# Both down projections as Strassen products over chunks of tile pairs

## The reference, cut to what matters

```
# first block, D_FF = 2816
x = x + (silu(h @ w_gate) * (h @ w_up)) @ w_down
x = rms_norm(x, final_norm)          # then second block's first rms_norm
# second block, D_FF_2 = 4096
f = square(relu(h @ w_ff1)) @ w_ff2
return x + rms_norm_2(f, g_post_ffn)
```

## Time and profile before

| | |
|---|---|
| median of 3 runs | 2897.8 us (2894.25 to 2903.49) |
| the profiled execution | 2899.71 us, of which the span of instructions is 2897.9 us |
| PE busy | 2785.0 us, 96% of the span, 13622 matmuls |
| DVE busy | 1349.2 us, 47% |
| POOL busy | 995.2 us, 34% |
| ACT busy | 842.6 us, 29% |
| mean granted PE clock | 0.975 |
| chain that ended last | PE 85%, DVE 6%, POOL 3% |

### The profile page before, as it was taken

The page is one execution under the profiler, slowest core; times in us unless marked ns, Lnnn a source line. Parts: engine busy times, 40 slices in busy tenths (PEclk is TensorE's granted clock), DMA queues, the critical chain, the costliest instruction groups (busy, mean ns, idle before and its releaser), DMA issues.

```text
span 2897.9 us, 34574 instructions
## 1 busy us (share of the span) xinstructions
PE 2785.0 (96%) x13622; PEld 2330.2 (80%) x13622; DVE 1349.2 (47%) x2385; ACT 842.6 (29%) x1584; POOL 995.2 (34%) x746
## 2 busy tenths in 40 slices
PE   7999999999999999999999899999996999999998
PEld 6767888777887888888788678989876888878887
DVE  4352111251233644444556621157627666656666
ACT  4352111122222423323121511057624233321121
POOL 2121100243233456555623432235244434322221
PEclk9899999999999999999999999989998999999999
DMA  4101220101341122222522122122023333333223
GB/s 164 49 34 45 90 71 32 62 15 48 107 170 66 67 87 79 81 88 99 214 88 95 67 75 67 40 63 60 19 96 99 99 115 111 134 141 108 96 88 102
DMA packets 104175, 248.28 MB, mean 86 GB/s; under 512 B 17829, under 2 KB 36901, under 8 KB 103845
## 3 DMA queue, kind: packets, MB, share of 16 engines
q1 hardware_dynamic: 104014, 246.07, 25.6%
HBM read 192.18 MB, written 53.59 MB: 85 GB/s over the span
## 4 chain that ended last, share of the span: by engine, by line
PE 85%; DVE 6%; POOL 3%; ACT 2%; issue 2%; DMA 1%; SPq 0%; POOLq 0%; DVEq 0%; ACTq 0%
PE PS L658 8%; PE PS L660 8%; PE PS L661 8%; PE PS L455 7%; PE PS L456 7%; PE PS L457 7%; PE PS L681 6%; PE PS L682 6%; PE PS L683 6%; PE PS L775 3%; PE PS L471 3%; PE PS L473 3%; PE PS L472 3%; PE PS L752 1%; PE PS L540 1%
## 5 line engine op out<-in xcount | busy, mean ns | idle before, releaser
L1781 POOL TENSOR_TENSOR WL<-WRAW,WH 128x1024 fp32r<-128x1024 f32 (+1 forms) x154 | 296.9, 1930 | 1063.2 <-ACT WH L828 1063.1
L828 ACT ACTIVATE WH<-WRAW 128x1024 fp32r<-128x1024 f32 (+1 forms) x262 | 223.6, 865 | 463.5 <-PE PS L683 374.8
L681 PE MATMUL PS<-WH,H1L 128*128 128x512 f32 x800 | 314.0, 393 | 9.9 <-DVE X L1554 9.6
L682 PE MATMUL PS<-WL,H1H 128*128 128x512 f32 x800 | 313.0, 391 | 0.0
L683 PE MATMUL PS<-WH,H1H 128*128 128x512 f32 x800 | 313.0, 391 | 0.0
L1556 DVE TENSOR_TENSOR X<-PS,X 128x512 f32<-128x512 f32 x368 | 242.6, 684 | 144.7 <-PE PS L683 138.4
L455 PE MATMUL PS<-HH,WL 128*128 128x512 f32 x736 | 294.2, 400 | 2.0 <-DVE HL L1268 1.9
L456 PE MATMUL PS<-HL,WH 128*128 128x512 f32 x736 | 291.3, 396 | 0.0
L457 PE MATMUL PS<-HH,WH 128*128 128x512 f32 x736 | 290.5, 395 | 0.0
L658 PE MATMUL PS<-HH,WL 128*128 128x512 f32 (+1 forms) x672 | 251.0, 373 | 8.0 <-DVE HS L1506 4.3
L660 PE MATMUL PS<-HL,WH 128*128 128x512 f32 (+1 forms) x672 | 249.4, 371 | 0.0
(11 more groups left out here) (336 smaller groups left out, 5527.7 us busy)
## 6 DMA issues: line engine op xcount, KB each, us to landing
WRAW<-in_u_f SPq DMA_DIRECT2D x64, 512.0 KB, 3.5
WRAW<-in_u_in SPq DMA_DIRECT2D x50, 512.0 KB, 3.5
HRAW<-scr_h SPq DMA_DIRECT2D x25, 1024.0 KB, 6.0
scr_h<-HS SPq DMA_DIRECT2D x96, 256.0 KB, 2.2
WRAW<-in_u_gu SPq DMA_DIRECT2D x44, 512.0 KB, 3.4
scr_x<-X SPq DMA_DIRECT2D x24, 512.0 KB, 3.0
WRAW<-in_u_dn SPq DMA_DIRECT2D x22, 512.0 KB, 3.5
X<-in_x SPq DMA_DIRECT2D x16, 512.0 KB, 8.4
```

Of the source, the lines that this page charges most:

```text
L681: e.matmul(PS[:, b, :], hl, wh, start=(t == ks[0] and f == 0), stop=False)
L682: e.matmul(PS[:, b, :], hh, wl, start=False, stop=False)
L1781: e.tensor_tensor(lo, raw, hi.bitcast(F32), ALU.subtract).then_inc(*c.inc("w_lo_p", i))
```

## The change

Both down projections become Strassen products. The tile pairs are taken in chunks: 3, 4 and 4 pairs in layer 1, four times 4 in layer 2. The hidden activation of a chunk is a 2x2 matrix of quarters A11 to A22 (rows 0 to 511 and 512 to 1023, first and second tile of each pair), and the weight likewise B11 to B22. For a chunk, SP loads the eight raw quarters straight from memory into `HHF` and `HLF` (the weights of this stage no longer pass through `WRAW`), 128x512 for each pair. POOL makes the eight sums S1 to S4 and T1 to T4 in place, for each pair (only S1 of the first chunk is made by DVE). For each of the seven products P1, P2, P5, P6, P7, P3, P4 and each pair of the chunk, ACT casts A and B (two instructions of 128x512) and DVE subtracts for both (two of 128x512). PE makes 4 groups of 3 matmuls for each pair, accumulated over the chunk in 4 banks. The A slots hold two products, so the split of a product waits until the product two before it is finished. DVE adds the finished banks into `X` or into a helper `DV` (28 additions of 128x512 for a chunk, from PSUM), and POOL adds `DV` into three of the four quarters of `X` and P1 into the fourth (16 instructions of 128x512 for a chunk, 12 in the first chunk of layer 2). In layer 1 the residual is loaded into `X` before. The last two products are made bank by bank, so that row tiles 0 to 3 finish with P3 and 4 to 7 with P4. The norm of layer 1 keeps its multiplication on POOL but has fewer small steps. In layer 2 POOL multiplies the row by the norm's weight (`XG`), and DVE then does scaling and residual in one instruction. The 324 fewer matmuls are 12 for each of 27 pairs.

```diff
+    CHUNKS = {1: [range(0, 3), range(3, 7), range(7, 11)], 2: [range(4 * k, 4 * k + 4) for k in range(4)]}
+    DORDER = ["P1", "P2", "P5", "P6", "P7", "P3", "P4"]
...
+        def ffn_down(lay):                        # PE
+            last = len(STEPS[lay])
+            for n, (k, p) in enumerate(STEPS[lay]):
...
+                    w.wait_ge(*c.at("d_al", (lay, n, i)))
+                    w.wait_ge(*lo_done(op))
...
+                    e.matmul(dst, hl, wh, start=(i == 0), stop=False)
+                    e.matmul(dst, hh, wl, start=False, stop=False)
+                    mm = e.matmul(dst, hh, wh, start=False, stop=(i == g - 1))
...
+                if n < last - 2:
+                    for i in range(g):
+                        for b in range(4):
+                            part(i, b)
+                else:
+                    for b in range(4):
+                        for i in range(g):
+                            part(i, b)
...
+        def d_split(lay, n, items):               # DVE
...
+            for i in items:
+                w.wait_ge(*c.at("d_ah", (lay, n, i)))
+                e.tensor_tensor(d_slot(lay, n, i, 1), d_tile(a_kind, i), d_slot(lay, n, i, 0).bitcast(F32),
+                                ALU.subtract).then_inc(*c.inc("d_al", (lay, n, i)))
+                op = DOP[lay, n, i]
+                w.wait_ge(*c.at("w_hi", op))
+                e.tensor_tensor(half_slot(WL, op), d_tile(b_kind, i), half_slot(WH, op).bitcast(F32),
+                                ALU.subtract).then_inc(*c.inc("w_lo_v", op))
...
+            for n in range(last - 1):
+                g = len(CHUNKS[lay][STEPS[lay][n + 1][0]])
+                for b in range(4):
+                    if n and STEPS[lay][n - 1][1] != "P1":
+                        add(n - 1, b)
+                    d_split(lay, n + 1, range(b, min(b + 1, g)))
...
+                def tile_sum(i, kind, left, right, sign):     # POOL
...
+                    e.tensor_tensor(d_tile(kind, i), d_tile(left, i), d_tile(right, i), sign).then_inc(
+                        *c.inc("d_s", (lay, k, i, kind)))
...
+                        e.tensor_tensor(d_out(q, b), d_out(q, b), DV[:, b, :], ALU.add).then_inc(
+                            *c.inc("d_v", (lay, k, q, b)))
...
+        def fin2(tt):                             # POOL
...
+            e.tensor_tensor(XG[:, tt % 2, :], X[:, tt, :], NG[:, 0, :], ALU.mult).then_inc(*c.inc("n_f", (6, tt)))
             rsqrt(6, tt, VV[1][:, tt:tt + 1], RR[1][:, tt:tt + 1])
...
+        def fin2(s):                              # DVE
+            if 0 <= s - 2 < NT:
+                finish(s - 2)
+            if 0 <= s - 1 < NT:
+                variance(6, s - 1, SS[1], VV[1])
```

More of the change, by code:

```diff
@@ L337, in ready @@
     def ready(i, key):
-        return all(p < NHS or bk.order.get(LAST.get(p - NHS), 1 << 30) <= bk.order[key] for p in places(i))
+        return ops[i][0] != "d" and all(p < NHS or bk.order.get(LAST.get(p - NHS), 1 << 30) <= bk.order[key] for p in places(i))
     def b_tile(kind, n):
@@ L666, in strassen @@
                         turns(k, backs, AFTER_PROD[lay][m][x])
[L668 to L695, removed]
@@ L697, in pe_program @@
         strassen(1, 2, backs)
-        ffn_down(1, FF1, "u_dn")
+        ffn_down(1)
+        for tt in range(4):
+            back(3, tt)
         for half in range(2):
@@ L703, in pe_program @@
                 proj_t(("zu", j, half), U["u_in2", j], half, HH, HL)
-                if half == 0 and j < 3:
-                    back(3, 5 + j)
+            if half == 0:
+                for tt in range(4, NT):
+                    back(3, tt)
         for tt in range(NT):
@@ L1234, in fin2 @@
         def fin2(tt):
-            w.wait_ge(*bk.out(("dl", 2, tt, 0)))
-            w.wait_ge(*bk.out(("dl", 2, tt, 1)))
+            if tt >= NT:
+                return
+            for done in row_done(2, tt):
+                w.wait_ge(*done)
             if tt >= 1:
@@ L2234, in ffn_down @@
             fin(-1)
+            w.wait_ge(*lo_done(DOP[lay, last - 1, len(CHUNKS[lay][-1]) - 1]))
+            feed(d_key(lay, last - 3, 3))
+            feed(d_key(lay, last - 2, 3))
             for tt in range(NT):
[L2236 to L2237 removed]
                 fin(tt)
+            feed(d_key(lay, last - 1, 3))
         def store_x2(tt):
```

580 lines of the change are left out of this document (351 added, 229 removed).

## The result

The changed kernel takes 2956.4 us (median; 2947.6 to 2957.1), the kernel before, in the same session, 2900.6 us: ratio 1.0188, 95% interval 1.0161 to 1.0216. The forecast was 2927 us (slower, 0.72). The direction and the mechanism were right, and the time lies in the range, but the cost was about twice what I forecast: 55.8 us instead of 29.2 (2927 against the 2897.8 us known then).

A forecast was written before the change was run, and what follows sets the result against it. PE alone bound the down stages before; DVE, delayed by POOL, would after. 2899.7 - 0.6 - 2.3 (stages) + 3 (loads) + 19.6 + 9.6 (layer ends) = 2929.0 us, median 1.9 lower: 2927 us; 8-in-10 range 2870 to 3000.

The forecast's parts named there:

- PE's saving: Down stages: 84 matmuls instead of 96 for each tile pair, 324 fewer at 0.2267 us, worth 73.4 us of PE.
- Chunk of four: Down stages: DVE's time for a chunk of four pairs, 51.2 + 52.3 - 12.2 = 91.3 us, above PE's 76.2.
- The price of a meeting: Down stages: a POOL instruction that meets a DVE subtraction costs DVE 1.70 - 0.61 = 1.09 us.
- the hidden additions: Down stages: 20 of DVE's 28 PSUM additions a chunk hidden behind waits for POOL, 12.2 us off.
- First chunks: First chunk of each layer on DVE: 72.6 us in layer 1, plus 3 us for loads, and 85.1 in layer 2.
- In the last chunk there is nothing to split during P4 ... 4.8 us off each: Last chunk of each layer: DVE's last 13.6 us shrink to PE's 8.8 us, 4.8 us off each stage.
- End of layer 1: After layer 1's down stage: PE stands 14.8 us instead of 5.2 while the norm's rows finish, +9.6 us.
- End of layer 2: Last norm: a POOL and DVE chain of 4.3 us a row ends 26 us after PE instead of 6.4, +19.6 us.
- A: Rival for the down stages: POOL and DVE find gaps for each other, PE stays the bound; 2824 us, chance 0.12.
- B: Rival for the down stages: all PSUM additions hidden, about as before, 2893 us; chance 0.14.
- C: Rival for the down stages: no addition hidden, +12.2 us in each of seven chunks, 3012 us; chance 0.12.
- D: Rival, the clock: short stops at every pair keep PE at its lower level, over 3200 us; chance 0.05.

The follow-up runs named there:

- sums narrow: Changed kernel with all but one column of each of GpSimd's 32 tile sums a chunk left out: 2844.8 us (one execution).
- copies: Changed kernel with each GpSimd sum of two tiles replaced by a copy of one of them, one SBUF input: 2836.2 us (one execution).
- The run by pair: Changed kernel with the last two products of each layer made pair of tiles by pair, not bank by bank: 2951.0 us (two executions 19 us apart).
- the kernel with all on VectorE: Changed kernel with GpSimd's 32 sums and 16 additions of `DV` a chunk moved to VectorE: 2887.2 us, ratio 0.9960 to the kernel before.
- the kernel with all on VectorE and the second unit later: Changed kernel with sums, `DV` additions and last norm's weight on VectorE, second weight feeding at layer 1's end later: 2879.1 us, ratio 0.9943 to the kernel before.
- the narrow additions: Changed kernel with all but one column of VectorE's 28 additions from PSUM a chunk left out: 2920.1 us (one execution).
- the kernel with the sums on VectorE: Changed kernel with the 32 tile sums a chunk moved from GpSimd to VectorE, `DV` additions kept on GpSimd: 2909.4 us, ratio 1.0027 to the kernel before.

## Why the prediction was right in kind and too small in size

- **PE's saving, 324 x 0.2267 = 73.4 us: right.** Where nothing holds PE up a chunk takes 76.1 us (sums narrow or copies).
- **Chunk of four, 91.3 us: right.** Measured 92.8, 91.6, 90.9, and 90.3 for the last of each layer up to its last split. The price of a meeting, 1.09 us, is that of the rows (1.77 - 0.68), and the hidden additions are worth the 12.2 us that I took off. First chunks: 75.6 and 89.2 us against 72.6 + 3 (for the loads) and 85.1; the 3 us for the loads fit in size, but no run separated them. In both first chunks DVE stands idle, which my sum had at nothing: in layer 2 for 10.1 us, 7.0 of them for ACT's casts of A and 3.1 for a raw quarter to land, in layer 1 for 7.2 us for the casts. In full chunks it never does. What of this makes the 4.1 us of layer 2 was not tested.
- **"In the last chunk there is nothing to split during P4 ... 4.8 us off each": the step that failed first.** VectorE's chunks sum to 258.7 and 361.9 us. PE started 6.7 and 6.0 us after the first split and ended 10.8 and 10.0 us after the last, so the stages came out 4.1 and 4.0 us above VectorE's sum, where I had them 4.8 below: +8.9 and +8.8 us. The diff says why: the last two products run bank by bank, the first bank of P4 needs the splits of all four pairs, and PE's 10.9 us for P4 cannot overlap them. I took the overlap from the pair-by-pair order of the other products; in that order PE does end earlier, 6.9 us after the last split. With 8.2 us from the last split to PE's end as the start of both norm chains, I then let the chains start from a point that was too early by the same error: the last split came 355.9 us after the stage's start, and my sum had it at 354.2 - 8.2 = 346.0. The run by pair shows that this point, not PE's end, decides.
- **End of layer 1, +9.6 us: measured +21.9, mis-sized.** The chain from the last split to the next product took 37.9 us, I had 23. 7.2 us are the second weight unit that all three engines split between the rows' norms (shown by feeding it later). The first one stands straight behind the last split (3.41 us at 1625.09; 1.22 us in the kernel with all on VectorE); that one was not moved in a run. In the kernel with all on VectorE and the second unit later 28.0 us are left, so the rows' chain itself is some 5 us longer than I had it. I had left the `feed` calls out of the sum; in a chain of small steps nothing covers them.
- **End of layer 2, +19.6 us: measured +21.0, right in sum.** The row's pace was 4.08 us (4.3 forecast). But I gave it all to GpSimd's multiplication, and only 7.3 us are that; in its absence VectorE's three wide instructions a row make 3.11 us, still slower than PE's 2.7. The sum came out partly by luck: from the last split to VectorE's last instruction it took 37.7 us where I had 34.4, but PE's end, from which the tail is counted, also came 1.8 us later behind that split.
- **Rivals.** A (the meetings don't decide) fell with the windows; it is what happens if those with the 32 sums cost 0.41 us. B and C, that all or no additions are hidden, fell with the narrow additions. D, the clock, did not come: 0.95 and 0.97 in the stages.
- **The marks I named** came nearly as written: subtractions with means of 1.11 and 1.64 us, GpSimd's sums with means of 1.69 to 1.74, DVE above 95%, PE at 86 and 89% (88 was my upper end), VectorE's last instruction 27.7 us after PE (some 20 named, 26 in the sum).

What is left of the difference is -6.5 us up to the first stage. The same code took 1363.7 to 1382.0 us there in the other versions of the changed kernel, so it can't be put down to the change; the granted clock was 0.95 instead of 0.90 from 60 to 160 us.

## What to carry to other kernels

An engine that is half idle is not free: price an instruction given to GpSimd by what it takes from VectorE (here its own length less 0.2 us for each meeting), and compare that with the 0.61 us for which VectorE does it itself. Sum a stage on the engine that bounds it, from its first instruction to its last, and then ask what must still run after that last one in the order of the loops; the next stage's chain hangs there. Work between the steps of a chain (here weights fed, 7.2 us) costs as soon as the chain is what everybody waits for.

## What the runs showed of the hardware

- **GpSimd's copy (one input) also holds up VectorE's subtraction (two inputs from SBUF),** for 0.41 us of its 0.61.
- **Wide instructions of 128x1024 with two inputs from SBUF behave the same:** VectorE's 1.28 us became 3.36 beside GpSimd's 2.35: 2.08 us of waiting, 0.27 less than GpSimd's length.
- **The clock changes equal stretches by 15 us.** In the second attention the changed kernel was granted 0.92 over 200 us, the kernel with the sums on VectorE, in the same stretch (from 200 us after the first product behind the pause), 1.00:

```profile
1863.00:2063.00 200.00, 198.94 (x1321) 187.51 (x1321) 104.29 (x368) 100.00 (x238) 66.92 (x56) 0.92 0.27 54
```

```profile
1854.00:2054.00 200.00, 198.94 (x1447) 189.44 (x1447) 115.69 (x409) 112.41 (x267) 74.26 (x63) 1.00 0.30 58
```

PE was busy for 198.94 us in both, and placed 1321 and 1447 matmuls in it. From the first product behind the pause to the down stage of layer 2 it is 894.9 us in the first and 879.8 in the second. The kernel before had 0.94 there, and 895.7 us. Kernels with the same code there took 879.5 us (narrow sums, copies) to 894.9, so it doesn't come with the code of the stretch. Each kernel was traced in one execution, so whether it goes by the kernel or by the execution stays open; it is why small effects are read here from stretches and not from whole times.
